# A transformer layer's MLP on one core: the first product in seven block products for eight, the second summed in PSUM

## What is computed

```python
mix_out = merged @ w_o[l]
x = layer_norm(ALPHA * x + g_m * mix_out, ln_mix_g[l], ln_mix_b[l])
u = layer_norm(x) * (1 + sc_f) + sh_f
h = jnp.square(jax.nn.relu(u @ w_ff1[l] + b_ff1[l]))
ff_out = h @ w_ff2[l] + b_ff2[l]
x = layer_norm(ALPHA * x + g_f * ff_out, ln_ff_g[l], ln_ff_b[l])
```

## Time and profile before

| | |
|---|---|
| median of 3 runs | 1620.14 us (1619.14 to 1620.56) |
| the profiled execution | 1619.49 us |
| its span, first to last instruction | 1617.7 us |
| mean granted TensorE clock | 0.987 of full |
| data moved by DMA | 108.51 MB |

### The profile page before, as it was taken

One profiled execution on the slowest core, in us unless ns is written; L12 is line 12 of the kernel. 1 busy time (PEld: TensorE's weight loads), 2 busy tenths in 40 slices (PEclk: granted clock), 3 DMA queues, 4 the chain that ended last, 5 costly groups with the idle time before them and its releaser, 6 DMA issues.

```text
span 1617.7 us, 17847 instructions
## 1 busy us (share of the span) xinstructions
PE 1536.9 (95%) x7162; PEld 1273.4 (79%) x7162; DVE 795.8 (49%) x1079; ACT 497.2 (31%) x726; POOL 111.8 (7%) x96
## 2 busy tenths in 40 slices
PE   6898999999979999999989799999999999999996
PEld 6687787887758888888778688888888888888885
DVE  4879688798672122224477632324232323324248
ACT  3312345554451111112336621304040312222132
POOL 1009200000000000000035100000000000000004
PEclk9999999999989999999999899999999999999998
DMA  9682101100001111132500220303020111102012
GB/s 346 206 271 93 35 20 34 34 27 14 27 14 52 52 52 39 52 104 84 190 1 1 80 77 10 96 0 93 10 78 26 52 52 46 58 26 78 0 52 104
DMA packets 110106, 108.51 MB, mean 67 GB/s; under 512 B 3624, under 2 KB 87774, under 8 KB 110056
## 3 DMA queue, kind: packets, MB, share of 16 engines
q1 hardware_dynamic: 110056, 107.82, 20.7%
HBM read 103.58 MB, written 4.23 MB: 67 GB/s over the span
## 4 chain that ended last, share of the span: by engine, by line
PE 85%; DVE 9%; ACT 3%; issue 2%; DMA 1%; POOL 0%; SPq 0%; ACTq 0%; DVEq 0%; POOLq 0%
PE ps L1368 25%; PE ps L1370 24%; PE ps L1369 24%; PE ps L1469 6%; PE ps L1388 2%; PE ps L1527 1%; DVE partial L981 1%; DVE mid L1067 1%; DVE bn L948 1%; DMA ada<-in_w_ada_dram 1%; DMA out_dram<-tmp 0%; PE ps L1671 0%; DVE w_lo L942 0%; ACT q_hi L619 0%; POOL tmp L591 0%
## 5 line engine op out<-in xcount | busy, mean ns | idle before, releaser
L1368 PE MATMUL ps<-act_hi,w_hi 128*128 128x512 f32 (+1 forms) x976 | 380.8, 390 | 3.7 <-DVE w_lo L1304 3.1
L1369 PE MATMUL ps<-act_lo,w_hi 128*128 128x512 f32 (+1 forms) x976 | 377.8, 387 | 0.0
L1370 PE MATMUL ps<-act_hi,w_lo 128*128 128x512 f32 (+1 forms) x976 | 377.6, 387 | 0.0
L1368 PEld LDWEIGHTS ps<-act_hi,w_hi 128*128 128x128 f32 x976 | 184.6, 189 | 42.0 <-DVE w_lo L1304 3.3
L1369 PEld LDWEIGHTS ps<-act_lo,w_hi 128*128 128x128 f32 x976 | 184.6, 189 | 37.3 <-issue 0.7
L1370 PEld LDWEIGHTS ps<-act_hi,w_lo 128*128 128x128 f32 x976 | 184.4, 189 | 37.0
L1368 PE MATMUL ps<-w_hi,h_hi 128*128 128x512 f32 x512 | 202.1, 395 | 0.0
L1369 PE MATMUL ps<-w_lo,h_hi 128*128 128x512 f32 x512 | 199.6, 390 | 0.0
L1370 PE MATMUL ps<-w_hi,h_lo 128*128 128x512 f32 x512 | 199.5, 390 | 0.0
L907 ACT ACTIVATE tmp<-ps,cols 128x1024 f32<-128x1024 f32 x32 | 35.7, 1116 | 490.6 <-PE ps L1370 490.6
L1312 DVE TENSOR_TENSOR mid<-mid,ps 128x1024 f32<-128x1024 f32 x63 | 76.9, 1221 | 205.6 <-PE ps L1370 201.7
...
## 6 DMA issues: line engine op xcount, KB each, us to landing
...
w_raw<-in_w_in_dram SPq DMA_DIRECT2D x42, 512.0 KB, 3.8
w_raw<-in_w_ff_dram SPq DMA_DIRECT2D x32, 512.0 KB, 4.7
row_raw<-in_w_ff_dram SPq DMA_DIRECT2D x32, 512.0 KB, 3.5
mid<-in_x_dram SPq DMA_DIRECT2D x16, 512.0 KB, 10.7
row_raw<-in_w_o_dram SPq DMA_DIRECT2D x8, 512.0 KB, 4.5
out_dram<-tmp SPq DMA_DIRECT2D x7, 512.0 KB, 2.6
...
```

What stands on the lines that cost most here:

```text
L1368: nc.tensor.matmul(out, sh, mh, start=first, stop=False)
L1369: nc.tensor.matmul(out, sh, ml, start=False, stop=False)
L1370: return nc.tensor.matmul(out, sl, mh, start=False, stop=last)
```

## The change

The first 4 feature blocks stay plain. The other 28 are made in 14 pairs. For a pair, the 1024 channels are halved, the 256 features are halved, and the 1024 tokens are halved, which makes a 2x2 by 2x2 block product, and that is made by Winograd's form of Strassen's scheme, seven products of 4 channel blocks x 3 passes each instead of eight. The token side's four sums (`t1_raw` to `t4_raw`) are made and cut once, at the entry to the MLP: two joins of high and low part on GpSimd (128x2048 each), two on VectorE, four subtractions on VectorE, then four high cuts and four low cuts; one of the sums takes the place of a quarter of `act_hi` and `act_lo` that is no longer needed. The weight side's four sums are made for each pair by `add_sums` on VectorE (4 x 128x512) and cut with the rest (`cut_set_hi`, `cut_sums_hi`, `cut_set_lo`, `cut_sums_lo`). The seven products go round all 8 PSUM banks; ScalarE saves the first (`save_first`), VectorE makes 7 additions (`post`), ScalarE does ReLU and square (`finish_h`), and SP stores h to DRAM (16 MB in all, plain blocks too).

The residual is spilled to DRAM at the entry (8 x 512 KB) and loaded back after the last product, since the cut weight sets need its place. Then the second product runs twice over all 32 feature blocks, once for each half of the tokens, four tiles in all eight banks, with no addition in between. For each block q of 64, SP loads 512 KB of w_ff2 and 256 KB of h (`load_k`, four raw buffers), VectorE scales the row (`scale_k`), ScalarE makes two high cuts (`cut_k_hi`), VectorE two low ones (`cut_k_lo`), into eight slots. The first four blocks of a half are taken by tile pairs and the last four tile by tile (`GATHER`). `take_tile` adds a finished tile to the residual. The tail (`norm_tile`, `finish_tile`, `last_tile`) is as before with other buffers. Nothing of the MLP is in a hardware loop any more.

```diff
-GROUP = 4
-GROUPS = D_FF // (P * GROUP)
+PLAIN = 4
+FF_BLOCKS = D_FF // P
+FF_PAIRS = FF_BLOCKS // 2
+FIRST_PAIR = PLAIN // 2
+PRODUCTS = 7
+RAWS = 4
+SLOTS = 8
...
+        def tile_bank(t):
+            return (6, 0, 2, 4)[t % 4]
+        def prod_bank(p, i):
+            return (prods_before(p) + i + 4) % 8
...
+            def load_pair(p):
+                if p < FIRST_PAIR + 2:
+                    if p == FIRST_PAIR:
+                        sp.wait_ge(res_done, ST)
+                        sp.wait_ge(x2_lo_done, ST - 1)
+                    else:
+                        sp.wait_ge(t_lo_done, 2)
+                else:
+                    sp.wait_ge(set_lo_done, sets_ready(p - 2))
+                sp.dma_start(pair_raw[p % 2][:, :, :], wff1_view[:, :, 2 * p * P:2 * (p + 1) * P])\
+                    .then_inc(pair_in[p % 2], 16)
...
+            def store_pair(p):
+                for i in range(2):
+                    sp.wait_ge(pair_sq, h_before(p) + 1 + i)
+                    sp.dma_start(h_dram[(2 * p + i) * P:(2 * p + i + 1) * P, :], h_buf[p % 2][:, i, :])\
+                        .then_inc(h_stored[p % 2], 16)
+            def load_k(q):
+                k, cs = q % FF_BLOCKS, slice(q // FF_BLOCKS * HALF, (q // FF_BLOCKS + 1) * HALF)
+                if q >= RAWS:
+                    sp.wait_ge(k_lo_done, q - RAWS + 1)
+                if q == PLAIN:
+                    for i in range(2):
+                        sp.wait_ge(h_stored[i], 32 * (FF_PAIRS - FIRST_PAIR) // 2)
+                sp.dma_start(w2_raw[q % RAWS][:, :], w_ff2[0, k * P:(k + 1) * P, :]).then_inc(k_in[q % RAWS], 16)
+                sp.dma_start(h_raw[q % RAWS][:, :], h_dram[k * P:(k + 1) * P, cs]).then_inc(k_in[q % RAWS], 16)
...
+            for t in range(ST):
+                sp.wait_ge(res_done, t + 1)
+                sp.dma_start(resid_rows[t], mid[:, t, :]).then_inc(spilled, 16)
+            for n in range(2, PLAIN):
+                sp.wait_ge(w_lo_done, N_FF0 + n - 1)
+                sp.dma_start(w_raw[n % 2][:, :, :], wff1_view[:, :, n * P:(n + 1) * P]).then_inc(w_arrived[n % 2], 16)
+            load_pair(FIRST_PAIR)
+            store_plain(0)
+            store_plain(1)
+            load_pair(FIRST_PAIR + 1)
+            store_plain(2)
+            store_plain(3)
+            for p in range(FIRST_PAIR, FF_PAIRS):
+                if p + 2 < FF_PAIRS:
+                    load_pair(p + 2)
+                if p == FF_PAIRS - 1:
+                    sp.wait_ge(set_lo_done, sets_ready(p))
+                    for n in range(2):
+                        sp.wait_ge(plain_stored[n], 16 * PLAIN // 2)
+                    for q in range(RAWS):
+                        load_k(q)
+                store_pair(p)
+            sp.wait_ge(prod_done, prods_before(FF_PAIRS))
+            sp.wait_ge(spilled, 16 * ST)
+            for t in range(ST):
+                sp.dma_start(resid[:, t, :], resid_rows[t]).then_inc(resid_in, 16)
+            sp.dma_start(ln_g2[:, :], ln_ff_g[0:1, :].partition_broadcast(P)).then_inc(ln_in, 16)
+            sp.dma_start(ln_b2[:, :], ln_ff_b[0:1, :].partition_broadcast(P)).then_inc(ln_in, 16)
+            for q in range(RAWS, FF_BLOCKS + SLOTS):
+                load_k(q)
...
+                if t == ST:
+                    pool.wait_ge(mix_done, ST)
+                    pool.wait_ge(x2_lo_done, ST // 2)
+                    for i, u in enumerate((t1_raw, t4_raw)):
+                        ks = slice(i * KT // 2, (i + 1) * KT // 2)
+                        nc.gpsimd.tensor_tensor(u[:, :, :], f(act_hi[:, ks, 0:HALF]), f(act_lo[:, ks, 0:HALF]), ALU.add)\
+                            .then_inc(u_joined, 1)
...
+            def cut_set_hi(p):
+                s = p % 2
+                act.wait_ge(pair_in[s], 16 * ((p - FIRST_PAIR) // 2 + 1))
+                if p == FIRST_PAIR:
+                    act.wait_ge(spilled, 16 * ST)
+                elif p == FIRST_PAIR + 1:
+                    act.wait_ge(f1_done, PLAIN)
+                    act.wait_ge(w_lo_done, N_FF0 + PLAIN)
+                else:
+                    act.wait_ge(prod_done, prods_before(p - 1))
+                copy(set_hi[s][:, 0:2, :, :].rearrange("p i k n -> p (i k) n"), pair_raw[s][:, :, 0:P])\
+                    .then_inc(set_hi_done, 1)
+                copy(set_hi[s][:, 2, :, :], pair_raw[s][:, KT // 2:, P:2 * P]).then_inc(set_hi_done, 1)
+            def cut_sums_hi(p):
+                act.wait_ge(s_added, 4 * (p - FIRST_PAIR + 1))
+                copy(set_hi[p % 2][:, 3:7, :, :], s_raw[:, :, :, :]).then_inc(set_hi_done, 1)
...
+            def cut_k_hi(q):
+                s, rs = q % SLOTS, q % RAWS
+                act.wait_ge(k_in[rs], 32 * (q // RAWS + 1))
+                if q < SLOTS:
+                    act.wait_ge(prod_done, prods_before(FF_PAIRS - 1 if q < 2 else FF_PAIRS))
+                else:
+                    act.wait_ge(k_used, q - SLOTS + 1)
+                copy(h_hi[s][:, :], h_raw[rs][:, :]).then_inc(k_hi_done, 1)
+                act.wait_ge(w2_scaled, q + 1)
+                copy(w2_hi[s][:, :], w2_raw[rs][:, :]).then_inc(k_hi_done, 1)
...
+            for n in range(2):
+                finish_plain(n)
+                cut_hi_into(n, ff_arrived(n + 2))
+            cut_t_hi(2, t_hi[2][:, :, :], t3_raw)
+            cut_t_hi(3, t_hi[1][:, :, :], t2_raw)
+            cut_set_hi(FIRST_PAIR)
+            finish_plain(2)
+            cut_sums_hi(FIRST_PAIR)
+            cut_t_hi(4, t_hi[3][:, :, :], t4_raw)
+            act.wait_ge(f1_done, PLAIN)
+            cut_t_hi(1, act_hi[:, 0:KT // 2, HALF:], t1_raw)
+            finish_plain(3)
+            for p in range(FIRST_PAIR, FF_PAIRS):
+                if p + 1 < FF_PAIRS:
+                    cut_set_hi(p + 1)
+                save_first(p)
+                if p + 1 < FF_PAIRS:
+                    cut_sums_hi(p + 1)
+                else:
+                    cut_k_hi(0)
+                    cut_k_hi(1)
+                finish_h(p, 0)
+                if p + 1 == FF_PAIRS:
+                    cut_k_hi(2)
+                    cut_k_hi(3)
+                finish_h(p, 1)
...
+            late = slice(HALF, SEQ)
+            for i, u in enumerate((t3_raw, t2_raw)):
+                ks = slice(i * KT // 2, (i + 1) * KT // 2)
+                if i == 0:
+                    dve.wait_ge(x2_lo_done, ST)
+                else:
+                    dve.wait_ge(x1_done, ST)
+                nc.vector.tensor_tensor(u[:, :, :], f(act_hi[:, ks, late]), f(act_lo[:, ks, late]), ALU.add)\
+                    .then_inc(u_joined, 1)
+            dve.wait_ge(u_joined, 4)
+            for i, (out, a, b) in enumerate(((t1_raw, t3_raw, t1_raw), (t3_raw, t2_raw, t3_raw),
+                                             (t2_raw, t2_raw, t1_raw), (t4_raw, t4_raw, t2_raw))):
+                nc.vector.tensor_tensor(out[:, :, :], a[:, :, :], b[:, :, :], ALU.subtract).then_inc(t_added, 1)
+                dve.wait_ge(t_added, i + 1)
+                if i in (1, 2):
+                    cut_plain_lo(i + 1)
...
+                nc.vector.tensor_tensor(s_raw[:, 0], a21, a22, ALU.add).then_inc(s_added, 1)
+                nc.vector.tensor_tensor(s_raw[:, 2], a11, a21, ALU.subtract).then_inc(s_added, 1)
+                dve.wait_ge(s_added, n + 1)
+                nc.vector.tensor_tensor(s_raw[:, 1], s_raw[:, 0], a11, ALU.subtract).then_inc(s_added, 1)
+                dve.wait_ge(s_added, n + 3)
+                nc.vector.tensor_tensor(s_raw[:, 3], a12, s_raw[:, 1], ALU.subtract).then_inc(s_added, 1)
...
+                prod, other, out = ((1, p1_copy, u2[:, :]), (2, u2, u4[:, :]), (3, u2, u3[:, :]),
+                                    (2, u3, h[:, 1, HALF:]), (4, p1_copy, h[:, 0, 0:HALF]),
+                                    (5, u4, h[:, 0, HALF:]), (6, u3, h[:, 1, 0:HALF]))[i]
...
+            cut_t_lo(1, t_lo[2][:, :, :], t3_raw, t_hi[2][:, :, :])
+            cut_t_lo(2, t_lo[1][:, :, :], t2_raw, t_hi[1][:, :, :])
+            add_sums(FIRST_PAIR)
+            cut_set_lo(FIRST_PAIR)
+            cut_sums_lo(FIRST_PAIR)
+            cut_t_lo(3, t_lo[3][:, :, :], t4_raw, t_hi[3][:, :, :])
+            cut_t_lo(4, act_lo[:, 0:KT // 2, HALF:], t1_raw, act_hi[:, 0:KT // 2, HALF:])
+            for p in range(FIRST_PAIR, FF_PAIRS):
+                if p + 1 < FF_PAIRS:
+                    add_sums(p + 1)
+                else:
+                    scale_k(0)
+                    scale_k(1)
+                post(p, 0)
+                if p + 1 < FF_PAIRS:
+                    cut_set_lo(p + 1)
+                post(p, 1)
+                if p + 1 < FF_PAIRS:
+                    cut_sums_lo(p + 1)
+                else:
+                    cut_k_lo(0)
+                    cut_k_lo(1)
+                    scale_k(2)
+                    scale_k(3)
+                for i in range(2, PRODUCTS):
+                    post(p, i)
+            cut_k_lo(2)
+            cut_k_lo(3)
...
```

(52 more changed lines are left out.)

397 lines of the change are left out of this document (244 added, 153 removed).

## The result

The change takes the median from 1619.82 us (4 runs) to **1593.38 us** (4 runs, 1591.82 to 1594.17): a ratio of 0.9836, 95% interval 0.9818 to 0.9853. That is a gain of 1.6%, clear of noise and less than 2%. It saves 26.4 us, 6.8 less than the 33.2 of the forecast, and 1593 lies inside the range. The profiled execution took 1593.42 us, its span is 1591.6.

The account below looks back on a forecast made before the run. The prediction took the kernel to be bound by TensorE's number of matmul instructions. Entry 0.8, slots -38.1, edges -5.5, seam 11.7 and tail -2.1 sum to -33.2 us, giving a median of 1587 us, range 1576 to 1603.

Parts of the forecast that it names:

- The slots and the edges: First product: 168 fewer 512-column matmul slots at 0.2269 us, -38.1 us; 21 waits on PSUM banks gone, -5.5 us.
- The pairs: Steady state of the 14 pairs: 19.06 us of TensorE each covers VectorE's 11.7 and ScalarE's 8.6; costed at nothing.
- Rivals C: Pairs: the round through the other engines, not TensorE, sets the pace at places; +13 us, 1600 us; chance 0.06.
- E: Whole kernel: TensorE's time does not follow its instruction count; 1619 us or so; chance 0.02.
- The seam: Between the two products: late posts 1.7, block 4 queued behind the residual burst 8.4, half-clock restart 1.6; +11.7 us.
- Rival A: Between the products: no loss, the burst ends before block 3 is used up; 1575 us; chance 0.09.
- the other end of the bounds: Between the products: loss of 21 us if the burst gets only 249 GB/s.
- The entry: Start of the MLP, up to block 2: joins and subtractions ahead of its weight cut on VectorE; +0.8 us, bounds -1.4 and +4.
- rival B: Entry and seam: GpSimd slows six VectorE passes, not two, or the burst gets 249 GB/s; 1597 to 1604 us; chance 0.14.
- The tail: End of kernel: VectorE's last addition comes 2.6 us after TensorE, not some 4.6; -2.1 us, bounds 0 and -4.
- The second product: Each feature block takes 5.45 us of TensorE, against a chain of about 3.8 us through VectorE and ScalarE.
- Rival D: Second product: the serial VectorE, ScalarE, VectorE hand-over per block sets the pace, slower than before; 1686 us; chance 0.05.

## Why the prediction was right, step by step

**The slots and the edges.** Forecast -43.6, found -44.1 with what is left over in the account's third row. The eighth product put back costs 38.4, which is the same term from the other side. The price of a slot, kept at 0.227, was kept rightly.

**The pairs.** Costed at nothing, and nothing was found: TensorE has no idle time in 28 blocks. Rivals C and E are out by this and by the eighth product.

**The seam.** Forecast 1.7 + 8.4 + 1.6 = 11.7, found 14.3: 12.4 of waits (0.8, 2.3 and 9.2, each rounded) and 2.0 of slower starts behind them. The mechanism was right at each place: late posts, the ReLU between the cuts, the burst ahead of block 4, the restart at half clock. The size was short. I had the last square end 9.5 us after the last product; it took 11.0 (from 1217.3 to 1228.31), as the posts, held behind the loads of blocks 0 and 1, then queued up. The burst took 19.3 us from its issue to VectorE's start (1228.75 to 1248.08) where I had 18.6; its rate was 382 GB/s for my 390. The restart of the earlier trace rows was 1.6, this one 1.7. I also missed the wait on a PSUM bank, 0.8 us with its interval taken off. The 358 GB/s of the Trainium skill (DMA: Bandwidth & Descriptors, Specifications) would have given 13.2 for the term, nearer to 14.3, but for the wrong reason: the rate measured was 382, and the lost time lay in the queue. Rival A (no loss) is out, and so is the other end of the bounds.

**The entry.** Forecast +0.8, found +3.3, within its bounds. The step that failed is "a VectorE pass of 1024 took 2.87 us ...; I add 1.5". I read the 2.87 as a pass slowed by GpSimd. It was a pass that waited: in the earlier trace rows GpSimd's row ends at 854.76, and the pass ends 1.08 us later, at 855.84. The price of that wait is not a share of VectorE's pass but what is left of GpSimd's, and GpSimd's joins are the longest instructions around. So in place of the 1.5 stood a 4.27, on a row of 0.16 that my sum left out and which stands ahead of the last x2 tile: it made the wait for the transposes 2.0 us longer. And VectorE's first join waited another 2.0 us for the residual row, which my forecast had near 911 to 914 and which ended at 916.96. Part of rival B (GpSimd holds up VectorE at the entry) was thus right in kind, at a third of its price. The Trainium skill (SBUF — State Buffer, Who interferes with whom) says that a VectorE instruction with two SBUF inputs contends with a GpSimd instruction that reads SBUF, and that whichever comes second is blocked for the whole of the first. The trace agrees, with 1.03, 4.27 and 8.58 us by the join's length.

**The tail.** Forecast -2.1, found -1.0, half of the term. VectorE's last addition came 3.7 us after TensorE's end, where I had 2.6. Again a `neg_mean` waits for GpSimd, 2.31 us beside a bias addition of 2.36. The kernel before had 1.13 at this place, and the difference of 1.2 is the size of the miss:

```profile
1578.86 2.36 POOL L705 TENSOR_TENSOR y_tmp<-y_tmp,ln_b 128x1024 f32<-128x1024 f32 x1 [3.02 <-DVE y_tmp L1656]
```

```profile
1578.94 2.31 DVE L1150 SCALAR_TENSOR_TENSOR neg_mean<-mean_var,rstd 128x1 f32<-128x1 f32 x1
```

```profile
1606.19 1.13 DVE L957 SCALAR_TENSOR_TENSOR neg_mean<-mean_var,rstd 128x1 f32<-128x1 f32 x1
```

(the last row is of the kernel before). This is read from rows only: the run that turned the order round gained nothing, so no run confirms it.

**The second product.** Rival D gave VectorE's contended 2.87 us for 1.22; nothing of it was seen, GpSimd being silent there. The two added passes show that its threshold is real and near: one more pass of 1.22 us per block is hidden, two are not.

**The sum of the misses:** seam +2.6, entry +2.5, tail +1.1, unchanged code +1.4, and -0.5 left over in the third row, together 7.1 for a difference of spans of 33.2 - 26.1. The four misses lie on one side, so the hit owes nothing to errors that cancelled: the range was wide enough for them. The seam's and the entry's have a cause that runs show, the tail's one that is argued. The unchanged code moves that much from one profile to the next, and what sets it stays open, as does why some kernels ran 13 or 14 starts at half clock where others ran 8.
